# Sixteen dense blocks of U in place of part of the U gathers, in a decoder layer with product-key experts

## What is computed

```
eid = i1 * N_KEYS + i2
g = jax.nn.softmax(best_s, axis=-1).astype(h.dtype)
a = jax.nn.gelu(jnp.einsum('td,thkd->thk', hx, expert_u[e]))
return jnp.einsum('thk,thkd->td', gw * a, expert_v[e])
x = _layernorm(ALPHA * h + _peer(h, ...), ln2_g, ln2_b)
```

## Time and profile before

| what | value |
|---|---|
| median of three runs | 1734.79 us (1731.76 to 1735.87) |
| profiled execution, its own time | 1734.55 us |
| its span | 1732.8 us |
| TensorE busy | 1363.6 us (79%) |
| VectorE busy | 1339.1 us (77%) |
| ScalarE busy | 654.9 us (38%) |
| GpSimd busy (issuing gathers for the most part) | 957.2 us (55%) |
| moved by DMA | 615.55 MB, mean 355 GB/s |
| first U gather, first V scaled, last dot | 461.5, 664.0, 1402.5 us |

### The profile page before, as it was taken

One profiled execution on the slowest core, in us unless ns is written; L12 is line 12 of the kernel. 1 busy time (PEld: TensorE's weight loads), 2 busy tenths in 40 slices (PEclk: granted clock), 3 DMA queues, 4 the chain that ended last, 5 costly groups with the idle time before them and its releaser, 6 DMA issues.

```text
span 1732.8 us, 19532 instructions
## 1 busy us (share of the span) xinstructions
PE 1363.6 (79%) x7442; PEld 1083.8 (63%) x7442; DVE 1339.1 (77%) x1907; ACT 654.9 (38%) x911; POOL 957.2 (55%) x591
## 2 busy tenths in 40 slices
PE   9999999999979913655555555577767799999976
PEld 8988999988668803554544455576667744444432
DVE  6666656666797999777757878887867877788898
ACT  5665456564201213344444544445557611000000
POOL 3210000000364677887787676788888455767782
PEclk9999999999989956677777787788888789999998
DMA  9876443466699999999999999999999999999997
GB/s 323 286 260 219 122 147 122 132 202 250 263 382 420 387 424 426 406 424 425 425 426 423 413 419 418 423 411 419 423 423 425 368 423 377 414 406 416 413 427 297
DMA packets 159390, 615.55 MB, mean 355 GB/s; under 512 B 20915, under 2 KB 74255, under 8 KB 96703
## 3 DMA queue, kind: packets, MB, share of 16 engines
q0 software_dynamic: 79232, 485.32, 68.2%
q1 hardware_dynamic: 80064, 128.99, 20.7%
HBM read 683.42 MB, written 2.10 MB: 396 GB/s over the span
## 4 chain that ended last, share of the span: by engine, by line
PE 28%; DMA 28%; POOL 17%; DVE 13%; issue 9%; ACT 3%; DVEq 2%; SPq 0%; POOLq 0%; ACTq 0%
DMA v_slot<-in_expert_v_dram,eid 22%; PE psum_all L596 14%; POOL u_slot L532 8%; POOL v_slot L551 7%; DVE u_slot L1825 7%; DMA u_slot<-in_expert_u_dram,eid 5%; PE psum_all L736 4%; PE psum_all L998 2%; POOL v_slot L554 2%; ACT v_slot L1321 1%; PE psum_all L761 1%; PE psum_all L717 1%; DVE xh L1861 1%; PE psum_all L623 1%; PE psum_all L621 1%
## 5 line engine op out<-in xcount | busy, mean ns | idle before, releaser
L1825 DVE SCALAR_TENSOR_TENSOR u_slot<-u_slot,xh 128x2048 f32<-128x2048 f32 x256 | 578.3, 2288 | 132.6 <-DMA u_slot<-in_expert_u_dram,eid 130.6
L998 PE MATMUL psum_all<-ident,v_slot 128*128 128x128 f32 x2304 | 389.5, 341 | 289.1 <-ACT v_slot L1321 288.9
L532 POOL DMA_INDIRECT u_slot<-in_expert_u_dram,eid x256 | 437.9, 1711 | 288.6 <-DVE u_slot L1825 116.0
L998 PEld LDWEIGHTS psum_all<-ident,v_slot 128*128 128x128 f32 x2304 | 350.7, 179 | 324.1 <-ACT v_slot L1321 319.8
L551 POOL DMA_INDIRECT v_slot<-in_expert_v_dram,eid x224 | 419.3, 1872 | 119.1 <-issue 65.1
L1321 ACT ACTIVATE v_slot<-v_slot,gate 128x2048 f32<-128x2048 f32 x144 | 287.4, 2000 | 319.8 <-DMA v_slot<-in_expert_v_dram,eid 319.6
L1861 DVE SCALAR_TENSOR_TENSOR xh<-v_slot,gate,xh 128x2048 f32<-128x2048 f32 x100 | 235.1, 2351 | 52.8 <-DMA v_slot<-in_expert_v_dram,eid 46.4
L1443 DVE TENSOR_TENSOR w_lo<-w_ring,w_hi 128x512 fp32r<-128x512 f32 x240 | 156.5, 687 | 79.9 <-ACT w_hi L1049 76.8
L596 PE MATMUL psum_all<-act_hi,w_hi 128*128 128x256 f32 x640 | 184.6, 289 | 1.1 <-DVE w_lo L1443 1.0
L596 PE MATMUL psum_all<-act_hi,w_lo 128*128 128x256 f32 x640 | 180.7, 282 | 0.0
L596 PE MATMUL psum_all<-act_lo,w_hi 128*128 128x256 f32 x640 | 180.6, 282 | 0.0
(11 more groups left out here) (296 smaller groups left out, 1688.0 us busy)
## 6 DMA issues: line engine op xcount, KB each, us to landing
w_ring<-in_w_in_dram SPq DMA_DIRECT2D x88, 512.0 KB, 4.8
u_slot<-in_expert_v_dram SPq DMA_DIRECT2D x40, 1024.0 KB, 8.7
wo_ring<-in_w_out_dram SPq DMA_DIRECT2D x32, 512.0 KB, 5.2
wq_ring<-in_w_query_dram SPq DMA_DIRECT2D x32, 512.0 KB, 10.4
w_ring<-in_cmp_k_w_dram POOLq DMA_DIRECT2D x16, 512.0 KB, 5.5
w_ring<-in_cmp_v_w_dram POOLq DMA_DIRECT2D x16, 512.0 KB, 4.2
u_slot<-in_expert_u_dram,eid POOLq DMA_INDIRECT x256, 19.6
v_slot<-in_expert_v_dram,eid POOLq DMA_INDIRECT x256, 18.6
```

Source lines behind the costliest of these rows:

```text
L532: nc.gpsimd.indirect_dma_start(out=u_slot[m % RU][:, :], out_offset=None, in_=expert_u[0], in_offset=bass.IndirectOffsetOnAxis(ap=eid[:, n ...
L998: ins = nc.tensor.matmul(bank[(4 if n < PH else 0) + c // 4][:, P * (c % 4):P * (c % 4) + P], v_slot[m % RV][:, P * c:P * c + P], ident[:, ...
L1825: V.scalar_tensor_tensor(u_slot[m % RU][:, :], u_slot[m % RU][:, :], 1.0, xh[:, n // PH, :], ALU.mult, ALU.mult, accum_out=u_dot[:, n, k:k ...
```

## The change

The 16 last first keys (112 to 127) are now left out of the U gathers too, by a bound, and out of the V gathers of units 14 and 15. For them SP loads the 16 blocks of U densely, 1 MB each, into `x_slot` (two slots, the homes of U slots 6 and 7). For a block `i` and a quarter of its columns, a step `j = 4 i + g`: TensorE transposes four 128 x 128 pieces (`u_transposes`), ScalarE copies them out (`u_out`), and TensorE multiplies them with `h` transposed, for both tiles at once, 256 columns (`u_dots`). After four steps `u_gelu` puts gelu of the products of that key with all tokens into `dense0` and `dense1x`, and `weigh` (VectorE) later multiplies them by the matrices of weights. The first 24 steps come before V 0 on TensorE and ScalarE; the other 40 go with V 0 to 39, one each. `h_transposes` makes the transposed `h` first.

Other parts: the U ring has 6 slots up to pick 125 and 8 from then on; the V ring 6 up to pick 89, then 7. `AHEAD` is 3, and the mix is 7 U to 5 V. ScalarE no longer does unit 2's exp and gelu ahead of the last query job. `gates_of` has six more small operations, so that picks with a skipped row count as zero. Two of the four loads of the second query-weight ring are issued earlier.

```diff
-AHEAD = 4
+RU_X = 6
+U_WIDE = 126
+RV_X = 6
+V_WIDE = 90
+RX = 2
+AHEAD = 3
+FX = 16
+X_FIRST = 24
-UNIT_AT = {(64 * (n - 3) + 4) // 5 + 4: n for n in range(4, 13)}
+UNIT_AT = {80 * n // 7 - 13: n for n in range(3, 13)}
...
+        def load_x_block(i):
+
+            first = NKEY * key_of(i)
+            sp.dma_start(x_slot[i % RX][:, :], expert_u[0][first:first + NKEY, :]).then_inc(s_xu[i % RX], 16)
+
+        sp.wait_ge(S["slot_used"], O(3, 7) + 1)
+        load_wq(1, 0)
+        load_wq(1, 2)
         sp.wait_ge(S["slot_used"], N_ITEMS)
...
-        for q in range(3):
-            load_wq(1, q)
+        load_wq(1, 1)
+        sp.wait_ge(S["t1_mm"], 4)
+        for i in range(RX):
+            load_x_block(i)
...
+        for i in range(RX, FX):
+            sp.wait_ge(S["ut_mm"], 4 * (i - RX + 1))
+            load_x_block(i)
...
-            nc.gpsimd.indirect_dma_start(out=u_slot[m % RU][:, :], out_offset=None, in_=expert_u[0],
-                                         in_offset=bass.IndirectOffsetOnAxis(ap=eid[:, n, k:k + 1], axis=0)
-                                         ).then_inc(s_u[m % RU], 16)
+            slot = u_ring(m)[0]
+            nc.gpsimd.indirect_dma_start(out=u_slot[slot][:, :], out_offset=None, in_=expert_u[0],
+                                         in_offset=bass.IndirectOffsetOnAxis(ap=eid[:, n, k:k + 1], axis=0),
+                                         bounds_check=ROWS_X - 1, oob_is_err=False).then_inc(s_u[slot], 16)
...
+            if RV_X <= m < V_WIDE:
+                pool.wait_ge(S["v_used"], m - RV_X + 1)
...
-            while sent < min(TOPK * NU, TOPK * AHEAD + (m + 1) * 5 // 4):
+            while sent < min(TOPK * NU, TOPK * AHEAD + (m + 1) * 7 // 5):
...
+        def u_dots(j):
+
+            i, g = divmod(j, 4)
+            pe.wait_ge(S["ut_ok"], j + 1)
+            if g == 0 and i:
+                pe.wait_ge(S["xa_ok"], i)
+            for c in range(4):
+                ins = nc.tensor.matmul(bank[2][:, 0:SEQ], uT[:, j % 2, c, :], hT2[:, 4 * g + c, :],
+                                       start=(g == 0 and c == 0), stop=(g == 3 and c == 3))
...
+        for i in range(2 * KC // 4):
+            h_transposes(i)
+        pe.wait_ge(S["hT_act"], 5 + 2 * KC // 4)
+        for j in range(X_FIRST):
+            u_transposes(j)
+            if j:
+                u_dots(j - 1)
         for m in range(PE_PICKS):
             n, k = divmod(m, TOPK)
+            j = X_FIRST + m
+            if j < 4 * FX:
+                u_transposes(j)
...
             ins.then_inc(S["v_used"], 1)
+            if j <= 4 * FX:
+                u_dots(j - 1)
...
-            if n in (5, 7, 8):
-                expo_gate((5, 7, 8).index(n))
-                gelu_unit((5, 7, 8).index(n))
+            if n in (5, 7):
+                expo_gate((5, 7).index(n))
+                gelu_unit((5, 7).index(n))
...
+        for i in range(2 * KC // 4):
+            h_out(i)
+        for j in range(X_FIRST):
+            u_step(j)
+            if j == 5:
+                unit(2)
...
+        def weigh(t, b):
...
+            V.tensor_tensor(cols, src[:, 0:FX, :], cols, ALU.mult).then_inc(S["weigh_ok"], 1)
```

More of the change, by code:

```diff
@@ L109, in chunk_loads, with key_of, ring, u_ring @@
     return n // 4 + (n % 4 >= 2)
+def key_of(f):
+    return NKEY - FX + f if f < FX else NKEY - FD + f - FX
+def ring(m, first, wide, at):
+    if m < at:
+        return m % first, m // first + 1
+    slot = m % wide
+    return slot, (m - at) // wide + 1 + (at // first if slot < first else 0)
+def u_ring(m):
+    return ring(m, RU_X, RU, U_WIDE)
+def v_ring(m):
+    return ring(m, RV_X, RV, V_WIDE)
 def kind_of(t):
@@ L284, in build @@
     u_slot = [at(f"u_slot{i}", [P, D], F32, u_home[i]) for i in range(RU)]
+    x_slot = [at(f"x_slot{i}", [P, D], F32, o_u + 8 * K * i) for i in range(RX)]
     v_slot = [at(f"v_slot{i}", [P, D], F32, v_home[i]) for i in range(RV)]
-    diag = at("diag", [P, TOPK, P], F32, oc + 56 * K)
-    sum0 = at("sum0", [P, KC, P], F32, oc + 56 * K)
+    diag = at("diag", [P, TOPK, P], F32, oc + 16 * K)
+    sum0 = at("sum0", [P, KC, P], F32, oc + 16 * K)
     sum1 = at("sum1", [P, KC, P], F32, oc + 48 * K)
@@ L326, in build @@
     s_u = [nc.alloc_semaphore(f"s_u{i}") for i in range(RU)]
+    s_xu = [nc.alloc_semaphore(f"s_xu{i}") for i in range(RX)]
     s_v = [nc.alloc_semaphore(f"s_v{i}") for i in range(RV)]
@@ L1392, in build_out, with h_out, u_out, u_gelu @@
             dense_out(1, b)
+        def h_out(i):
+            t, c0 = divmod(4 * i, KC)
+            act.wait_ge(S["yt_mm"], 9 + i + 1)
+            nc.scalar.activation(hT2[:, c0:c0 + 4, P * t:P * t + P], bview(i % 2, 4, P), ACT.Copy).then_inc(S["hT_act"], 1)
+        def u_out(j):
+            act.wait_ge(S["ut_mm"], j + 1)
+            nc.scalar.activation(uT[:, j % 2, :, :], bview(j % 2, 4, P), ACT.Copy).then_inc(S["ut_ok"], 1)
+        def u_gelu(i):
+            act.wait_ge(S["xs_mm"], i + 1)
+            nc.scalar.activation(dense0[:, i, :], bank[2][:, 0:P], ACT.Gelu_apprx_tanh)
+            nc.scalar.activation(dense1x[:, i, :], bank[2][:, P:SEQ], ACT.Gelu_apprx_tanh).then_inc(S["xa_ok"], 1)
+        def u_step(j):
+            if j < 4 * FX:
+                u_out(j)
+            if j > 4 and j % 4 == 1 and j <= 4 * FX + 1:
+                u_gelu(j // 4 - 1)
         def unit(n):
-            expo_gate(n)
+            if n < 12:
+                expo_gate(n)
             gelu_unit(n)
         act.wait_ge(S["eps2_ok"], 1)
-        unit(3)
+        for i in range(2 * KC // 4):
[4 more added lines that the diff above has]
+                unit(2)
         for m in range(PE_PICKS):
@@ L1402, in _ @@
                 unit(UNIT_AT[m])
+            if m == LATE_AT:
+                for n in range(12, NU):
+                    expo_gate(n)
             if m == V0_PICKS + 1:
@@ L1823, in dot, with late_weights @@
             m = TOPK * n + k
-            dve.wait_ge(s_u[m % RU], 16 * (m // RU + 1))
-            V.scalar_tensor_tensor(u_slot[m % RU][:, :], u_slot[m % RU][:, :], 1.0, xh[:, n // PH, :], ALU.mult, ALU.mult,
+            slot, uses = u_ring(m)
+            dve.wait_ge(s_u[slot], 16 * uses)
+            V.scalar_tensor_tensor(u_slot[slot][:, :], u_slot[slot][:, :], 1.0, xh[:, n // PH, :], ALU.mult, ALU.mult,
                                    accum_out=u_dot[:, n, k:k + 1]).then_inc(S["dots_done"], 1)
+        def late_weights():
+            for n in range(NU - 2, NU):
+                i = n - NU + 2
+                dve.wait_ge(S["exp_ok"], n + 1)
+                V.reciprocal(g_inv[:, n:n + 1], g_sum[:, n:n + 1])
+                dve.drain()
+                V.tensor_scalar(w_late[:, i, :], b_val[:, n, :], g_inv[:, n:n + 1], None, ALU.mult)
+                dve.drain()
+                V.scalar_tensor_tensor(b_val[:, n, :], b_id[:, 0, n, :], float(NKEY - FX), w_late[:, i, :], ALU.is_ge, ALU.mult)
+            dve.drain()
@@ L1908, in _ @@
                 m = TOPK * n + k
+                if (n, k) == (13, 12):
+                    late_weights()
                 if m in HOT0_AT:
                     hot_rows(0, HOT0_AT[m])
+                if m in WEIGH0_AT:
+                    weigh(0, WEIGH0_AT[m])
                 if m in HOT1_AT:
@@ L1914, in _ @@
             hot_rows(1, b)
+        for b in (NG_T - 2, NG_T - 1):
+            weigh(1, b)
         V.tensor_scalar(xh[:, 1, :], xh[:, 1, :], ALPHA, None, ALU.mult)
```

183 lines of the change are left out of this document (119 added, 64 removed).

## The result

The changed kernel takes **1771.73 us** (median of 4, 1768.09 to 1772.92) against 1734.66 for the kernel before (4 runs): a ratio of 1.0214, with an interval of 1.0199 to 1.0229. That is 37 us slower, where the forecast was 12 us slower with a range up to 1770. The profiled execution took 1768.09 us; its span is 1766.4 us.

A forecast was written before the change was run, and what follows sets the result against it. DMA bytes were taken as the bound, VectorE close behind. From 692 us, five dot stages sum to 723, so dots end at 1415, against 1402.5; 1734.55 + 12 = 1746.5 us, range 1719 to 1770.

The forecast's parts named there:

- What bounds the kernel: From 461 to 1643 us the DMA engines set the pace, at 407 to 418 GB/s; VectorE is next.
- V 0 and the gap: 24 block steps delay the first V slot to 687 us (was about 668); GpSimd idles 40 to 55 us before.
- The 36 us saved are spent by 687 us on a dry queue: At 687 us, 279 MB remain before and after the change, so the net 14.5 MB saved gives no lead.
- Dots 57 to 105: First stage after the gap, with 8 of 16 blocks: 73.9 MB, 185 us by DMA, 3 added for TensorE: 188.
- Dots 105 to 137: Second stage, at DMA's 3.44 us per dot with before's shortfall of 2 to 3%: 113 us.
- Dots 137 to 177 and 177 to 216: VectorE's 3.50 and 3.54 us per dot against DMA's 3.44; taken as 3.55 and 3.6: 142 and 140 us.
- Dots 216 to 256: Last dots: 51 MB, 128 us by DMA; with `weigh` and the peak in the hot rows, 140 us.
- The final stage: After the last dot, TensorE's 40 dense blocks and VectorE's tail repeat 330 us, minus 1 for thinner last V rows.
- The bytes did not win: Rival: steps at full clock, stages at the DMA limit, total 1719 or 1729 us; chance 0.28 for 1716 to 1731.
- Exact cancelling: Rival: same bytes left at 687 us and the same pace as before, 1732 to 1740 us; chance 0.15.
- The slow clock: Rival: the 24 steps run at clock 0.50, total 1764 or in full 1800 us; chance 0.15, shared with GpSimd's issue rate.
- GpSimd's pace: Rival: one gather issued per 2.21 us, 337 left at 687 us, total 1769 us; chance 0.15, shared with a slow clock.

The follow-up runs named there:

- Experiment 9: Kernel before with each dot over 1024 of the 2048 columns, so half of every dot product is left out: 1723.68 us, ratio 0.9943.
- experiment 12: Kernel before, U rows of the last 16 first keys not gathered (from gather 8 on), no dense blocks instead, their dots left out: 1702.73 us, ratio 0.9797.
- experiment 1: Changed kernel with exp and gelu of units 3 to 12 five V picks earlier in ScalarE's program: 1759.8 us, ratio to before 1.0142.
- 10: Changed kernel with the gather order of before and each dot over 1024 of the 2048 columns: 1712.91 us, ratio 0.9881.

## Why the prediction was right on the sign and too small

- **What bounds the kernel: held for dots 72 to 245.** Experiment 9 shows it more sharply than the trace of before did. Before dot 72 it did not hold: experiments 9 and 12 show VectorE there.
- **V 0 and the gap: held in kind.** Forecast: V 0's transposes at 680 to 690 us, first slot back at 687, GpSimd idle for 40 to 55 us. Measured: 675.3, 677, 37.83. A step takes 0.60 us of transposes and 1.89 of products, of which 0.3 overlap, so 2.17, not 2.27; the clock was granted at 1.00 all the way, and the 3 us for 0.91 were not due. DMA moved 109 GB/s in 650 to 680 us and 136 in 650 to 685, above the mark of 100; three blocks of 1 MB were issued from 652.7 to 672.7 us.
- **"The 36 us saved are spent by 687 us on a dry queue": held for this kernel, and it hid the other half.** Dot 57 came at 687, where I had 692. But I had credited 36 us to bytes at a flat rate, and experiment 12 shows that the bytes saved before dot 72 buy nothing in a kernel without a gap either. The gap spent a saving that was partly not there.
- **Dots 57 to 105, 188 us: 193 measured.** That dot 105 came at 880, as forecast, is luck: the start came 5 us sooner.
- **Dots 105 to 137, "32 x 3.44, with before's shortfall of 2 to 3%: 113": failed.** Measured 122. The formula knows DMA alone, and here VectorE waited twice for about 10 us for the exp of a unit, which stands behind a V pick on ScalarE. That is not all of it: with those waits gone in experiment 1, the stage still took 120 us, in the old order 122. The DMA moved 46 MB in it (122 us at 399 GB/s), where the formula has 44.
- **Dots 137 to 177 and 177 to 216, 142 and 140: 145 and 143.** VectorE's wait for U there fell from 42 us to 1.4, as forecast (under 15). Its work per dot was 3.47 in dots 145 to 177 (3.50 forecast) and 3.48 in dots 177 to 216 (3.54). What came on top of the work was 12 us of waits for ScalarE, not the two servers in bursts that I had allowed for.
- **Dots 216 to 256, 140: failed.** Measured 151. I took bytes, `weigh` and a peak; VectorE's work was 3.1 per dot, it never waited for U, and 19.4 us of waits for ScalarE stand there (13.7 at L2028, 5.7 at L1984).
- **The final stage, 330 minus 1: 325.3**, 4 us better.

So the step that failed is the sum "from 692 us to the last dot": 723 us forecast, 754 measured from 687 (the dots end at 1441, not 1415). Of the 31 us, 5 lie in dots 57 to 105, 9 in dots 105 to 137, 6 in dots 137 to 216 and 11 in dots 216 to 256. I had asked of each stage whether DMA or VectorE was slower, and nowhere what VectorE waits for besides U: the waits for ScalarE, 77 us in all, are a term that the sum does not have.

Most of them come from the places of the units. Before, unit 4 stood behind V 16 on ScalarE, and its `gates_of` (after dot 90) found 21 V gathers issued ahead of U 90. Now unit 4 stands behind V 31, and only 30 V gathers are issued ahead of U 90. A lead of four V picks has become a lag of two. The forecast read the new order for GpSimd and not for ScalarE.

Experiment 1 puts 12 us on the places of the units. The other 13 or so of the 25 between 1746.5 and 1771.7 are not shown one by one. The rate of the gathers, 390 to 401 GB/s from 1002 to 1290 us where I had taken 0.40 MB per us, which is 419, is no cause of them, since VectorE waited only 1.4 us for U there.

**The rivals.** The bytes did not win: they needed VectorE under 3.4 us of work per dot, and it had 3.47 and 3.48. Exact cancelling fits the time of the old order (1737.16), not of this one, and there too by a saving of 35 against a cost of 38, not by equal bytes. The slow clock didn't come (0.96 to 1.00 through the steps). GpSimd's pace gave 1769, next to the measured 1771.7, but not by its mechanism: from 684 to 1441 us GpSimd itself waited 88.0 us for dots (L588 behind L1960) and was busy 101 of 145 and 114 of 143 us in the two stages from 1002 to 1290, where it should have been full. The number agreed by chance. The premise about its gathers does hold, though the 0.95 us that I read as "VectorE idle" fell beside the small operations of `ids`; in the gap of the changed kernel, with VectorE idle, a gather took 1.00. In 700 to 900 us GpSimd was busy 165.04 us on 97 instructions before (1.70 each), and with half dots:

```profile
700.00:900.00 200.00, 113.11 (x652) 100.02 (x651) 88.75 (x218) 91.55 (x56) 104.57 (x93) 0.78 1.01 425
```

104.57 on 93, 1.12 each; it just wasn't the bound, since dots 72 to 245 went no faster for it. The Trainium skill, GPSIMD Engine Reference, section 1 (Specifications), says that GpSimd shares its SBUF interfaces with VectorE, with contention where an instruction of VectorE has two SBUF inputs. The trace agrees.

No complete version tried beats the kernel before (experiments 9, 10 and 12 leave part of the work out). The nearest, the changed kernel in the old gather order, is level with it, 0.15% slower.

## What to carry to other kernels

Price saved bytes stage by stage: they are worth their transfer time only where the transfers set the pace, and bytes put in their place are paid where they are loaded. When an in-order queue holds gathers for two consumers, find the first gather that waits for a slot, and ask when that slot comes back and how many of the other kind are issued ahead of it; here 15 gathers decided between 421 and 109 GB/s. And when an order changes, follow every pair of a producer and a consumer on different engines through it, not only the queue that was reordered; but price a new wait by trying it away, since a new order with 85 us of waits cost 7 us in one kernel, and 55 us of waits taken away gave 12 in another.
